# GpSimd adds squares and makes three weight rests between an expert layer and a retention projection

## The reference, cut to what matters

```
out = sum over 16 experts of gate * ((silu(tok @ w1) * (tok @ w3)) @ w2)      # expert layer of layer 0
hc, h = hc + g2c * out[:256], h + g2 * out[256:]                              # residual, 512 tokens
xm = modulate(h * rsqrt(mean(h * h) + eps) * norm_g, sh1, sc1)                # norm of layer 1
ql, kl, vl, gl = split(xm @ w_in)                                             # retention projection
```

## Time and profile before

| | us |
|---|---|
| median of three runs | 1726.11 |
| the profiled execution's own time | 1729.55 |
| its span | 1727.8 |
| PE busy (matmuls) | 1664.8 |
| DVE busy | 1154.4 |
| ACT busy | 1007.5 |
| POOL busy | 64.1 |

### The profile page before, as it was taken

One profiled execution on the slowest core, in us unless ns is written; L12 is line 12 of the kernel. 1 busy time (PEld: TensorE's weight loads), 2 busy tenths in 40 slices (PEclk: granted clock), 3 DMA queues, 4 the chain that ended last, 5 costly groups with the idle time before them and its releaser, 6 DMA issues.

```text
span 1727.8 us, 29945 instructions
## 1 busy us (share of the span) xinstructions
PE 1664.8 (96%) x12171; PEld 1429.4 (83%) x12179; DVE 1154.4 (67%) x1591; ACT 1007.5 (58%) x1333; POOL 64.1 (4%) x66
## 2 busy tenths in 40 slices
PE   6999999999999999999999899999989999999998
PEld 4787676888888868888989688888878998897688
DVE  5332874798989984343366698998976587545564
ACT  4422763588888875224344588888865573454561
POOL 0000000000000010000000000000010000100100
PEclk9999999999999999999999999999999999999999
DMA  8645215899999963223564499999974554274512
GB/s 338 219 129 235 113 50 207 330 389 401 402 409 408 392 249 134 97 98 143 198 267 185 176 397 402 403 403 408 398 292 147 195 185 158 73 235 156 166 55 74
DMA packets 52556, 419.79 MB, mean 243 GB/s; under 512 B 16980, under 2 KB 18132, under 8 KB 30048
## 3 DMA queue, kind: packets, MB, share of 16 engines
q1 hardware_dynamic: 26416, 364.56, 53.6%
q0 software_dynamic: 8304, 31.64, 6.0%
q10 hardware_dynamic: 17728, 22.02, 3.8%
HBM read 398.23 MB, written 19.97 MB: 242 GB/s over the span
## 4 chain that ended last, share of the span: by engine, by line
PE 83%; DVE 8%; DMA 4%; ACT 2%; issue 2%; POOL 0%; SPq 0%; ACTq 0%; DVEq 0%; POOLq 0%
PE ps L767 50%; PE ps L913 17%; DMA ring<-w_all 4%; PE ps L728 3%; DVE w_lo L2335 2%; PE ps L751 2%; PE ps L922 1%; PE ps L1153 1%; PE ps L1164 1%; PE ps L1179 1%; PE ps L929 1%; DVE arena L2274 1%; PE ps L774 1%; PE ps L807 1%; PE ps L1368 1%
## 5 line engine op out<-in xcount | busy, mean ns | idle before, releaser
L2335 DVE TENSOR_TENSOR w_lo<-ring,w_hi 128x1024 fp32r<-128x1024 f32 x384 | 452.2, 1219 | 48.2 <-ACT w_hi L1669 46.6
L1669 ACT ACTIVATE w_hi<-ring 128x1024 fp32r<-128x1024 f32 x384 | 397.0, 1058 | 99.4 <-PE ps L913 57.4
L767 PE MATMUL ps<-XT_lo,arena_r 128*128 128x256 f32 (+1 forms) x1712 | 386.0, 301 | 2.4 <-DVE arena L3007 1.1
L767 PEld LDWEIGHTS ps<-XT_lo,arena_r 128*128 128x128 f32 x1712 | 283.1, 191 | 17.9 <-issue 3.5
L913 PE MATMUL ps<-w_hi,x_hi 128*128 128x256 f32 (+1 forms) x768 | 249.0, 324 | 7.6 <-DVE w_lo L2335 3.9
L913 PE MATMUL ps<-w_hi,x_lo 128*128 128x256 f32 (+1 forms) x768 | 244.4, 318 | 0.0
L913 PE MATMUL ps<-w_lo,x_hi 128*128 128x256 f32 (+1 forms) x768 | 244.4, 318 | 0.0
L767 PE MATMUL ps<-arena_r 128*128 128x512 f32 (+1 forms) x656 | 233.1, 363 | 8.4 <-DVE arena_r L2511 3.8
L767 PE MATMUL ps<-XT_lo,ring_r 128*128 128x256 f32 x640 | 180.7, 282 | 0.0
L2189 DVE TENSOR_TENSOR ring_r<-ring,arena_r 128x1024 fp32r<-128x1024 f32 x96 | 114.0, 1221 | 96.3 <-ACT arena_r L1570 96.2
L913 PEld LDWEIGHTS ps<-w_hi,x_hi 128*128 128x128 f32 x768 | 145.8, 190 | 26.7 <-DVE w_lo L2335 9.2
(11 more groups left out here) (385 smaller groups left out, 2637.3 us busy)
## 6 DMA issues: line engine op xcount, KB each, us to landing
ring<-w_all SPq DMA_DIRECT2D x172, 2048.0 KB, 9.7
y_d<-arena ACTq DMA_DIRECT2D x30, 512.0 KB, 9.9
arena<-toep_d POOLq DMA_DIRECT2D x16, 384.0 KB, 12.1
arena<-rpb ACTq DMA_DIRECT2D x16, 192.0 KB, 3.8
xtok_d<-arena ACTq DMA_DIRECT2D x6, 512.0 KB, 3.0
hT<-h SPq DMA_DIRECT2D x2, 1024.0 KB, 6.0
arena<-cb_d POOLq DMA_DIRECT2D x1, 1536.0 KB, 12.0
arena<-cc_d POOLq DMA_DIRECT2D x1, 959.0 KB, 9.5
```

Of the source, the lines that this page charges most:

```text
L767: last = nc.tensor.matmul(out, a, b, start=(first and i == 0), stop=(final and i == 2))
L1669: nc.scalar.activation(w_hi[:, q], slot(b, "p (q c) -> p q c", q=4)[:, q], ACT.Copy).then_inc(hi_rdy, 1)
L2335: nc.vector.tensor_tensor(w_lo[:, q], slot(base + n, "p (q c) -> p q c", q=4)[:, q], as_f32(w_hi[:, q]), ALU.subtract).then_inc(*split_sig ...
```

## The change

On layer 0 and routed experts alone, the eight rows of squares become three for PE, and four rests are shared out:

- POOL, behind its gathers, adds the squares of rows 1 to 5 one after another into row 0, each add waiting for its square and for the add before; then it makes the rests of units 1, 2 and 3, each as soon as ACT's high half is there. All eight count `nm_part`.
- PE runs the residual loop without the norm's products. Then `norm_pooled` sums row 6, waits for the fifth add (`nm_part` 7), sums row 0 (which holds rows 0 to 5) and then row 7. `warm` stays behind it. The projection's units 1, 2 and 3 wait for `nm_part` 8, 9 and 10.
- ACT squares all eight rows first, then makes high halves 0 and 1, takes the root, and makes halves 2 and 3 behind it.
- DVE makes rest 0 alone, behind the last residual row. Behind the norm's eight rows it waits for `nm_part` 10 and raises `dw_lo` by three, so that later counts stay as they were.
- `norm_part(3)` waits for 11 in place of 3.

```
--- before.py
+++ after.py
...
                 by_load(pool, layer, gather, ungather)
+                if layer == 0:
+                    sq = squares_of(2)
+                    for m in range(1, 6):
+                        pool.wait_ge(nm_sq, KT * 2 + m + 1)
+                        if m > 1:
+                            pool.wait_ge(nm_part, 2 + m - 1)
+                        nc.gpsimd.tensor_tensor(sq[:, 0], sq[:, 0], sq[:, m], ALU.add).then_inc(nm_part, 1)
+                    for p in range(1, 4):
+                        pool.wait_ge(dw_hi, DW_RET + p + 1)
+                        nc.gpsimd.tensor_tensor(part_of(B_RET, p, False, ring_r), part_of(B_RET, p, False, ring),
+                                                as_f32(ret_hi(p)), ALU.subtract).then_inc(nm_part, 1)
...
+            def norm_pooled():
+
+                norm_sum(2, 6, first=6)
+                pe.wait_ge(nm_part, 7)
+                nc.tensor.matmul(ps[:, 7, 0:T], ones, squares_of(2)[:, 0], start=False, stop=False)
+                norm_sum(2, 7, first=6)
...
-                    if m >= 3:
-                        norm_after(layer, m - 3)
...
+                if layer == 0:
+                    norm_pooled()
+                    warm(3, 14)
...
                     if k == 0:
-                        pe.wait_ge(dw_lo, DW_RET + m + 1)
+                        pe.wait_ge(*((nm_part, 7 + m) if m else (dw_lo, DW_RET + 1)))
...
-                    if layer == 0 and m >= 4:
-                        ret_split(m - 4)
-                if layer == 1:
+                if layer == 0:
+                    ret_split(0)
+                    ret_split(1)
+                else:
                     z_split(0)
                 norm_roots(layer)
-                if layer == 1:
+                if layer == 0:
+                    ret_split(2)
+                    ret_split(3)
...
-                    if layer == 0 and m in (5, 6, 7):
-                        ret_split(m - 5)
-                    if layer == 0 and m == 7:
-                        ret_split(3)
+                if layer == 0:
+                    ret_split(0)
...
+            dve.wait_ge(nm_part, 10)
+            dve.sem_inc(dw_lo, 3)
             for p in range(4, 6):
                 ret_split(p)
```

More of the change, by code:

```diff
@@ L776, in norm_sum, with norm_after @@
                     last.then_inc(nm_ms, 1)
[L778 to L783, removed]
+            def norm_after(k):
+                norm_sum(4, k, weight=sum_w[:, k:k + 1].broadcast_to([P, P]))
+            def norm_pooled():
[3 more added lines that the diff above has]
+                norm_sum(2, 7, first=6)
             def norm_part(i):
                 a, b = NORM_COLS[i]
-                pe.wait_ge(nm_part, (1, 2, 0, 3)[i])
+                pe.wait_ge(nm_part, (1, 2, 0, 11)[i])
                 nc.tensor.matmul(ps[:, 7, 0:b - a], ones, squares_of(i)[:, 0], start=True, stop=False)
@@ L1013, in routed @@
                     last.then_inc(f_c, 1)
-                    if m >= 3:
-                        norm_after(layer, m - 3)
-                for k in range(KT - 3, KT):
-                    norm_after(layer, k)
-                if layer == 1:
+                    if layer == 1 and m >= 3:
+                        norm_after(m - 3)
+                if layer == 0:
+                    norm_pooled()
+                    warm(3, 14)
+                else:
+                    for k in range(KT - 3, KT):
+                        norm_after(k)
                     norm_plain()
-                else:
-                    warm(3, 14)
             def dense(layer):
@@ L1028, in dense @@
                 experts(layer)
-                for k in range(KT):
-                    norm_after(layer, k)
-                if layer == 1:
+                if layer == 0:
+                    norm_pooled()
+                else:
+                    for k in range(KT):
+                        norm_after(k)
                     norm_plain()
@@ L2439, in dense @@
                 if layer == 0:
-                    for p in range(4):
-                        ret_split(p)
+                    ret_split(0)
                 dve.sem_inc(dve_step, after - steps[0])
```

## The result

The changed kernel takes **1732.22 us** (median of 20 runs, 1728.56 to 1738.59), the kernel before 1727.06 beside it (20 runs, 1722.83 to 1732.54): ratio 1.0024, 95% interval 1.0016 to 1.0033. It is about 4 us slower by the ratio, whose interval does not hold 1; the forecast was 1.7 us faster, and the time lies above the range, though still in the band of 0.3% that was given 0.89. The execution profiled after the change took 1730.58 us, with a span of 1728.7; against the profiled execution of before that is only 1.03 us more, and why a pair of profiles shows so little of it is part of what follows.

What follows compares the result with a forecast made beforehand. PE, 83% of the chain that ended last, was taken to bound the kernel; an earlier root gained 1.67 us, all other terms nothing: 1726.11 less 1.67 is 1724.4 us, range 1721.5 to 1730.0.

Steps and rivals of the forecast that it cites:

- The loop: Residual loop without PE's norm products and DVE's rests: last residual half ends at 630.37 against 634.01.
- Five adds: POOL's chain of adds into row 0, from 626.25 at 1.29 us each, ending at 632.70.
- I take the same stretch at the lower level as before, so nothing: PE's low-clock stretch around the projection's first 27 products stays as before, costing or gaining nothing.
- Rival D: PE's clock falls early, in the new quiet; two norm products at half speed lose 1.8 us: 1726.2 us; chance 0.08.
- I take that each runs at its own rate: Behind the root, POOL's rests and DVE's work do not hold each other up: no cost.
- Rival A: POOL's rests shut out DVE's multiply and rest of x; first product 1.64 us later, 1727.75 us; chance 0.32.
- B: POOL's first add starts late, behind a possible fetch; root 3.95 us later than before, 1730.1 us; chance 0.12.
- C: PE's clock stays up at the projection's first products; 2.75 us more gained, 1721.7 us; chance 0.08.

Runs made afterwards that it cites:

- e3: Changed kernel plus 13 useless TensorE products between row 6's product and the wait for the pooled sum; ratio 1.0000 to the kernel before.
- e2: Changed kernel without the GpSimd adds: TensorE sums all eight rows in the loop, GpSimd only makes the three rests; ratio 1.0023 to the kernel before.
- e4: Changed kernel with all four high halves of the weight made ahead of ScalarE's root; ratio 0.9992 to the kernel before.
- g4: Changed kernel with the three rests moved from GpSimd back to VectorE, all else as changed; ratio 1.0009 to the kernel before.
- e1: Changed kernel with only the adds on GpSimd: halves and rests made by ScalarE and VectorE between the rows as before; ratio 1.0001 to the kernel before.
- a0: Changed kernel run again unchanged, for a second profile; ratio 1.0024 to the kernel before.
- w1: Kernel before with 20 useless TensorE products in place of 14 ahead of the projection; ratio 0.9983 to the kernel before.
- g1: Changed kernel with useless TensorE products in both quiet spells: 13 ahead of the pooled sum, 31 for 14 ahead of the projection; ratio 0.9990 to the kernel before.
- g2: Changed kernel with three GpSimd adds, all rests on VectorE, 6 useless TensorE products ahead of the expert paths' join and 17 behind; ratio 0.9990 to the kernel before.
- h: Same as g2 but with 7 useless TensorE products behind the join in place of 17; 1722.82 us, ratio 0.9964 to the kernel before.
- f: Changed kernel with three GpSimd adds in place of five, all rests on VectorE, 20 useless TensorE products ahead of the projection; ratio 0.9998 to the kernel before.
- b0: Kernel before run again unchanged, for a second profile; its handover ended at 30.86 us.

## Why the prediction was wrong

**The loop: right.** The last residual half was put at 630.37 in the time of before; with 0.98 added it ended at 630.25.

**Five adds: the price right, the collision missed.** "I take the middle, 1.29 an add": one add takes 1.28. The steps are 1.43, 0.15 of it from one add to the next, which four steps make 0.6. The fifth add lost 0.96 more (2.24 against 1.28) to VectorE's rest 0, which the prediction had put at "nothing". The chain ended at 634.24 in place of 632.70, 1.54 late.

**"I take the same stretch at the lower level as before, so nothing": failed.** The low clock came earlier, under the sum's product and row 7's. Rival D was right about the two products: 1.98 us more than the 1.80 planned, 1.80 of it the clock (e3) and the rest a price that was a little low. Sum: 1.67 early as forecast, less 1.54, less 1.98 is 1.85 late, and the root was 1.85 late (14.22 against 12.37).

**"I take that each runs at its own rate": failed.** Rival A happened at its place: GpSimd's rests, 2.35 each (2.49 was forecast), held the multiplies, and root to first product grew by 2.59, to 7.22; A had put it at 7.94. e2, e4 and g4 tie this to GpSimd's rests: the multiplies take 5.10, 1.15 and 0.76 with two whole rests, a quarter of one, and none of them beside. e1 and g4 show the same between GpSimd's adds and VectorE's rests, in both directions. The rule of the Trainium skill (SBUF — State Buffer, "SBUF: two separate sides") agrees with these rows; the reciprocal, with one tile read, took 1.75 with GpSimd's rest beside it or not.

**One rival at a time.** The range was built from cases priced one by one. A and D came together: by the prediction's own prices 1726.11 less 1.67 plus 3.31 plus 1.80, or 1729.6, still inside the range. With the 1.54 of the adds it is 1731.1, outside. The forecast held neither A nor D nor the late adds, and each rival at most one of them. Before itself came out 0.95 higher beside the changed kernel (1727.06) than the 1726.11 that the forecast starts from.

**B fell:** the first add started 0.09 us behind square 1 (625.32 against 624.60 plus 0.63). If the extra row stands for a load, none of it showed on the path.

**C came in part, and by chance:** in the first profile of the changed kernel the projection runs at 1.00, in the second its first products run at 0.50. C's reason against itself, idle spells as long as before, did not hold: the one ahead of the projection was 3.02 and 3.84 in place of 1.65.

**What the loss is made of.** By the chain the first product is 4.44 later. What the projection gives back depends on the clock: 4.20 us in the first pair of profiles, 1.0 in the second. The mean granted clock over the runs says which is nearer: 0.9922 in the 12 runs of a0, 0.9944 in the 29 of before beside them, 0.9956 in w1 and 0.9961 in g1. A line through the runs of each of these kernels gives 1.1 to 1.6 us for 0.001 of clock, so that, as an estimate, 2.3 to 3.4 of the 4 us go with the clock, and the rest with the chain at an equal clock. g1, which fills the quiet spells and leaves the rests on GpSimd, undoes all of it. The ratios say also that the parts do not add up: the rests alone cost all of the loss (e2, 1.0023) and the adds alone nothing (e1, 1.0001), each with about 0.0013 either way, yet with both in place it goes when the first quiet spell is filled (e3, 1.0000) or when the rests come ahead of the multiplies (e4, 0.9992).

**Open:** how often the second low stretch comes in the changed kernel, and how often before has one at all; I have two profiles of each. Low stretches elsewhere in the kernel, where nothing was changed, come and go as well: by windows of 2 us over the span, without the handover and the last 5 us, they make 6.8 us in the profile of e1 and 27 in that of e2, so that one pair of profiles says little of 4 us. The chain alone should have left g1 slower than w1 by 2.6 us; the two ratios differ by 1.2, with intervals as wide. What TensorE waits for at the join no run was made to find.

## What to carry to other kernels

Before work goes to GpSimd, list the two-input instructions of VectorE that will run at the same time: on these tiles each one waited until the other's had ended, 2.6 us for an instruction of 0.4 in e2. Count the quiet spells of TensorE that a change makes, and fill all of them; in w1 six more products of no use were worth 2.9 us. And take a second profile before a stretch of low clock is read as a constant of the kernel: here it was half as long in the second profile.

## What the runs showed that I had not expected

The low clock moves rather than goes: with one quiet spell filled (e3) it appears behind the next, with both filled (g1) it is gone. In every handover that has one, it began during an idle spell of TensorE of 1.6 to 5 us or within 1.5 us of its end; nine of the eleven stretches last 6.8 us and two 3.4. Not every such spell brings one: the stall of 2.26 in g2 and that of 2.97 in h did not. And its place matters: e1, e4 and g4 have it under the last products of the norm, where it costs 1.8 us on two of them (e3), and not under the projection, where the first profile of before lost 2.75.

TensorE stands still for 2.26 and 2.97 us where the two paths of the expert layer join, with no releaser in the profile, in the two runs in which it gets there early (g2, h). In w1, which gets there later, only 0.36 us are left ahead of the first product, and these have a releaser. TensorE's timeline of g2:
```profile
634.06 1.46 PE L747 MATMUL ps<-cst 128*128 128x512 bf16 x6
637.78 3.84 PE L747 MATMUL ps<-cst 128*128 128x512 bf16 x17 [2.26 <-issue]
641.27 0.47 PE L774 MATMUL ps<-arena_r 128*128 128x256 f32 x1
```
The 2.26 stands ahead of the first filler behind the join, and no other engine's row ends there. The DMA rows have something, though: the queue that they list as q8, "instruction", moves one packet of 0.02 MB at 635.27 in g2, and the fillers start 2.51 us later. It does so ahead of each longer gap that TensorE has there without a releaser: the products go on 2.75 us behind such a packet in h, 2.68 in f, 2.45 in before and 2.26 in b0, and the late first product of f stands 2.73 behind another. In w1 such a packet, at 639.89, has no gap behind it. A wait for instructions is likely by this, and not shown.
